# Modulation fillers placed otherwise: three in each mLSTM head, three in each RWKV pair

## What is computed

```
mod = silu(c) @ w_ada + b_ada            # six parts of 2048 columns each
h   = rmsnorm(x) * (1 + sc_a) + sh_a
z   = h @ w_in
y   = concat(rwkv7(z_a), mlstm(z_qk, z_rest)) @ w_out
x   = x + g_a * y
h   = rmsnorm(x) * (1 + sc_c) + sh_c
x   = x + g_c * peer(h)
mod = silu(c) @ w_ada_final + b_ada_final  # two more parts
y   = rmsnorm(x) * (1 + scale) + shift
```

## Time and profile before

| | us |
|---|---|
| median of 3 runs | 3099.91 |
| lowest and highest | 3097.11, 3103.96 |
| the profiled execution | 3092.3 |
| its span | 3090.5 |
| PE busy in the span | 2778.7 (90%) |
| POOL busy | 1741.7 (56%) |
| DVE busy | 1275.7 (41%) |
| ACT busy | 988.4 (32%) |

### The profile page before, as it was taken

The page is one execution under the profiler, slowest core; times in us unless marked ns, Lnnn a source line. Parts: engine busy times, 40 slices in busy tenths (PEclk is TensorE's granted clock), DMA queues, the critical chain, the costliest instruction groups (busy, mean ns, idle before and its releaser), DMA issues.

```text
span 3090.5 us, 57072 instructions
## 1 busy us (share of the span) xinstructions
PE 2778.7 (90%) x22999; PEld 2568.8 (83%) x22999; DVE 1275.7 (41%) x2183; ACT 988.4 (32%) x1350; POOL 1741.7 (56%) x719
## 2 busy tenths in 40 slices
PE   5689999958875979998999999899999899889997
PEld 1389996526653979998999899899999899889997
DVE  0350664464226640995788713200131201352233
ACT  1243432131102333444444333233333233223323
POOL 0167771002211757688455577677777677777774
PEclk9699997779986989999999999999999999999999
DMA  9534446966661434344444444455444454444442
GB/s 355 224 141 163 163 163 233 325 218 241 236 244 78 151 122 163 123 163 149 143 168 172 150 164 159 149 186 187 165 156 166 170 186 180 164 152 165 152 164 99
DMA packets 153351, 544.47 MB, mean 176 GB/s; under 512 B 9080, under 2 KB 22024, under 8 KB 124168
## 3 DMA queue, kind: packets, MB, share of 16 engines
q1 hardware_dynamic: 136384, 505.18, 46.0%
q10 hardware_dynamic: 14680, 20.41, 1.9%
q0 software_dynamic: 2160, 17.03, 1.3%
HBM read 518.74 MB, written 23.84 MB: 176 GB/s over the span
## 4 chain that ended last, share of the span: by engine, by line
issue 32%; POOL 28%; PE 25%; DVE 8%; DMA 5%; ACT 1%; POOLq 0%; SPq 0%; ACTq 0%; DVEq 0%
POOL ring_lo L561 28%; PE bank L627 25%; DMA kept<-in_w_ada 4%; DVE staged L1580 1%; DMA kept<-in_w_adaf 1%; DVE staged L1865 1%; DVE staged L1525 1%; DVE staged L1854 0%; ACT hi_front L1183 0%; DVE staged L1736 0%; ACT staged L1183 0%; DMA out_n_all<-staged 0%; DVE staged L1539 0%; POOLq L560 0%; DVE staged L1985 0%
## 5 line engine op out<-in xcount | busy, mean ns | idle before, releaser
L561 POOL TENSOR_TENSOR ring_lo<-kept,hi_peer 128x1024 fp32r<-128x1024 f32 x576 | 1444.4, 2530 | 623.8 <-ACT hi_peer L1183 623.8
L1183 ACT ACTIVATE hi_peer<-kept 128x1024 fp32r<-128x1024 f32 x576 | 578.9, 1053 | 1231.3 <-PE bank L627 1231.1
L627 PE MATMUL bank<-h_hi,ring_lo 128*128 128x288 f32 x3104 | 917.0, 295 | 0.0
L627 PE MATMUL bank<-h_hi,hi_peer 128*128 128x288 f32 x2304 | 690.3, 300 | 36.9 <-DVE staged L1865 15.9
L627 PE MATMUL bank<-h_lo,hi_peer 128*128 128x288 f32 x2304 | 684.1, 297 | 0.0
L627 PE MATMUL bank<-act_hi,hi_peer 128*128 128x288 f32 x2048 | 616.3, 301 | 41.0 <-POOL ring_lo L561 16.0
L627 PE MATMUL bank<-act_lo,hi_peer 128*128 128x288 f32 x2048 | 609.9, 298 | 0.0
L627 PE MATMUL bank<-act_hi,ring_lo 128*128 128x288 f32 x2048 | 609.7, 298 | 0.0
L627 PEld LDWEIGHTS bank<-h_hi,ring_lo 128*128 128x128 f32 x3104 | 589.2, 190 | 0.0
L627 PEld LDWEIGHTS bank<-h_hi,hi_peer 128*128 128x128 f32 x2304 | 436.4, 189 | 40.2 <-issue 35.7
L627 PE MATMUL bank<-staged 64*64 64x64 f32 (+10 forms) x5472 | 371.6, 268 | 91.6 <-issue 20.0
(11 more groups left out here) (186 smaller groups left out, 2442.5 us busy)
## 6 DMA issues: line engine op xcount, KB each, us to landing
kept<-in_peer_u SPq DMA_DIRECT2D x128, 1024.0 KB, 4.8
kept<-in_peer_v SPq DMA_DIRECT2D x128, 1024.0 KB, 5.6
kept<-in_w_ada SPq DMA_DIRECT2D x96, 1024.0 KB, 8.8
kept<-in_w_in SPq DMA_DIRECT2D x50, 1024.0 KB, 4.7
kept<-in_w_adaf SPq DMA_DIRECT2D x32, 1024.0 KB, 8.8
kept<-in_w_out SPq DMA_DIRECT2D x16, 1024.0 KB, 4.8
kept<-in_w_q SPq DMA_DIRECT2D x16, 1024.0 KB, 4.7
gates_spill<-staged ACTq DMA_DIRECT2D x32, 432.0 KB, 2.7
```

The source lines that it names most:

```text
L561: pool.tensor_tensor(ring_lo[:, n % RING_SLOTS, cols], ring[n % RING_SLOTS][:, cols], hi_slot(n)[:, cols].bitcast(F32), ALU.subtract).then ...
L627: return pe.matmul(out, lhsT, rhs, start=start, stop=stop)
L1183: return act.activation(out, in_, ACT.Copy)
```

## The change

In each head a third filler is put behind `ms_ready`, ahead of the state updates; on ScalarE its counterpart stands behind the root. In each pair the two fillers behind levels 1 and 3 become one behind level 2, and the one at the end of the pair is gone. The sum stays at 24, and the last stays in the sample part.

```diff
@@ TensorE, mLSTM head @@
                 for i in range(2):
                     mm = matmul(ps[0][:, 0:N], ones, hsq[:, i, :], i == 0, i == 1)
                 mm.then_inc(S("ms_ready"), 1)
+                ada_more(1)
 
                 pe.wait_ge(S("kwm_ready"), h + 1)
@@ TensorE, RWKV pair, levels of the doubling @@
                             times(q, q, X, Tt).then_inc(S("t_sum"), 1)
-                    if i == 1 or i == 3:
+                    if i == 2:
                         ada_more(1)
@@ TensorE, end of the pair @@
                     mm.then_inc(S("y_sum"), 1)
-                ada_more(1)
```

## The result

The kernel with the change takes 3116.86 us in the median of five runs (3111.45 to 3120.76), beside 3097.68 us for the kernel before (3096.22 to 3103.96). The ratio is 1.0052, with a 95% interval from 1.0037 to 1.0067: slower by 16 us. Two later series of the same kernel, each beside its own runs of before, gave 1.0083 (1.0067 to 1.0099, median 3124.4) and 1.0071 (1.0050 to 1.0092, median 3121.5). The change thus costs 16 to 26 us, and the forecast was +8. The direction was right, the first series lies in the range of 3098 to 3120, the medians of the two others just above it.

A forecast was written before the change was run, and what follows sets the result against it. It took waits for modulation-weight loads, a tile every 2.72 us, to bound the third fillers in the heads. Heads +44.0 and pairs -36.1 made +8 us, so 3108 us from a median of 3099.9; range 3098 to 3120.

The forecast's parts named there:

- The bound and the rate: Heads: a filler directly behind another waits for its tiles, landing every 2.72 us, and ends some 12 to 14 us later.
- The heads: Four third fillers ahead of the state updates delay them by 11.4, 11.3, 11.0 and 10.3 us, together 44 us.
- the clock rival: Heads: waits leave TensorE's clock low, each following head costs 3.5 us more, 10 together: 3118 us; chance 0.2.
- The fold "beside the loads, at nothing": Head 1, between second and third filler: the moved fold costs nothing beside the loads; 4.2 us without that cover.
- The pairs: RWKV pairs with four fillers less: -36.1 us together, bounds -31 to -38; pair 0 17 and pair 1 19 us shorter.
- the copy: End of pair 0: without the filler, the next products need only ScalarE's copy of the output, -7.2 us.
- the sample's filler: Behind pair 1: it still waits a little for tiles, ending near 903.8 against 918.90 us; 15.1 of 15.3 us kept.
- The other side: Rival in the heads: third fillers find their tiles and cost matmuls plus one fold, 19 to 26 us: 3085 to 3093; chance 0.1.
- Nothing to be seen: Rival: heads cost 40 us and pairs give 38, so 3102 us; chance 0.2.
- The signs: Expected in the trace: heads 10 to 12 us longer, last state near 669 us; new level 1 waits or numerators over 10 us refute.
- the 1.94 us that I called the lower clock: Heads: one tile's matmuls at the lower clock, upper end for the 1.5 us charged for the last tile.
- Behind the heads: Between the heads and the pairs: one filler and one fold beside the last state's stores, costed at nothing, perhaps a few microseconds.

The follow-up runs named there:

- Kept busy: Changed kernel plus two constant matmuls before the third filler's second to fourth tiles: heads 0 and 3, 3115.3 us (1.0067); heads 0, 2, 3, 3116.3 us (1.0054).
- the run of the pairs alone: Changed kernel without the heads' third fillers, four quarters of the modulation and their loads left out: 3059.1 us beside 3093.6 for the kernel before, ratio 0.9889.
- the run with unloaded fillers: Changed pairs, four quarters left out, plus 16 filler-shaped matmuls on constants per head at the third filler's place, no load: 3080.4 us.

## Why the prediction was right, and where its size was off

**The bound and the rate** were right for the gap between two fillers. The third filler's tiles arrived when the rows of before said (last group of head 0 at 526.39, predicted landing 526.9), and without a load the same matmuls cost the heads 16.4 us instead of 57.7.

**The heads: 44 us forecast, 57.7 measured in the first trace, 66.6 and 69.6 in the next two.** This is the term that was mis-sized. It ended at the start of the updates and took everything behind it as unchanged. The first series' 3116.9 lies nearer to the clock rival's 3118 than to the forecast of 3108. Per head the first trace has +14.5, +13.5, +14.5 and +15.2 against 11.4, 11.3, 11.0 and 10.3. In heads 0 and 3 the updates start 11.5 and 11.6 us later, counted from the head's start; the rest is the updates at 1.2 GHz, 9.23 us instead of 6.25 and 5.58. Kept busy, head 0 took 39.1 (37.4) and head 3 40.3 (43.8), where the forecast makes 38.1 and 40.7: in three of these four the sum without the clock holds within about 1 us. In head 2 the third filler ends where the forecast has it, within about 0.5 us once the fold that left the head's first filler is taken off, and the fold and the updates behind it make the difference (the kernel after, merged into one row; 4.2 and 5.71 us, 9.9 together, in the forecast):

```profile
619.46 12.95 PE L627 MATMUL bank<-staged 128*128 128x9 f32 x52
```

The 66.6 and 69.6 us of the later traces also hold more low clock ahead of the wait. Part of that spread comes without any third filler: the run of the pairs alone had heads of 130.6 us together, with two fillers, where the trace of before has 124.1.

**The fold "beside the loads, at nothing"** in head 1 failed in the same way, by its clock. TensorE's order of time in head 1, the kernel after:

```profile
562.63 1.06 PE L627 MATMUL bank<-kept,staged 128*32 128x512 f32 x8 [0.77 <-DMA kept<-in_w_ada]
563.62 5.79 PE L627 MATMUL bank<-staged 128*128 128x9 f32 x32
569.26 2.27 PE L627 MATMUL bank<-staged,kept 128*128 128x288 f32 x4
572.35 5.04 PE L627 MATMUL bank<-kept,staged 128*32 128x512 f32 x32 [0.82 <-issue]
577.32 5.59 PE L627 MATMUL bank<-staged 32*128 32x257 f32 x20
```

At the low clock the fold takes 5.79 us and the sum of squares 2.27 instead of 1.24. The filler no longer waits for tiles; its matmuls come in one piece behind the landed load and end 2 us later than they would have beside it. The pause of 0.82 us ahead of it, which the profile calls issue, fits the wait for the folded result that I had named: ScalarE's copy of it ends at 572.25.

**The clock as a rival** was named, with 3118, and it is what happened, at 13.7 us in the first trace instead of 10. I had given it 0.2 because the heads ran at the low level for part of their time before. That argument was weak: a stretch that is already slow in part leaves the rest to be lost. I had also put its price in the wrong place, the next filler and numerator, where it was the updates directly behind the wait. The Trainium skill ("TensorE: Matmul & The Clock Gate", section "HAM oscillation — how this bites in real kernels") describes waits for DMA between short bursts that send the engine back to its low clock; these traces agree, with a granted clock of 0.50 in the stretch behind the wait.

**The pairs: -36.1 forecast.** Measured -35.5 in the trace of that part alone; in the change -39.5 up to the sample products (19.0 in pair 0 and 20.5 in pair 1, forecast 17 and 19), with 2.1 given back. The parts stand: no wait opened behind the missing filler, the copy was next at the end of pair 0, and the sample's filler kept a small price.

**The other side** (a third filler that finds its tiles, 3085 to 3093) is what the run with unloaded fillers stands for: with free loads it came out below before, 3080 beside 3093.6, though 8 of these 13 us are the unexplained ones behind the start of `w_out`. With real loads it did not come. Its price was also added up wrongly: 19 to 26 against -36.1 makes 3083 to 3090, not 3085 to 3093. **Nothing to be seen** needed heads of 40.

**The signs.** The last state is handed to its store at 682.7 us instead of 625.3; I had said near 669. No new wait stands at the doubling's filler, and no numerator takes over 10 us (6.4 to 8.9). One reading of mine was loose: the 1.94 us that I called the lower clock stand where the profile gives a granted clock of 1.00 (from 36 to 40 us). Nearly the same, 1.93 us, stand at 526.39, where it gives 0.50, so the size holds; why the first row reads 1.00 stays open.

**Behind the heads** the stretch from head 3's end to the pairs was 98.0 us before and 98.2 after, so costing it at nothing was right.

## What to carry to other kernels

A filler has two prices, its matmuls and its bytes, and they are hidden in different places: look for a stretch where another engine is the bound *and* the transfers stand still. Count the bytes over the whole period of a loop, not over the gap between two fillers, and price them at the average rate of that period (here 300 to 330 GB/s), not at the rate of a full queue (385). A wait put ahead of small matmuls cost more than its length here, because what followed ran at half the clock; charge the work behind it at its low-clock duration.

## What the runs showed of the hardware that was not expected

- The same kernel's four heads took 181.8, 190.7 and 193.7 us in three executions, with the same matmuls at the low clock for more or less of their time (head 0's numerator 6.41 to 8.88 us), while the last tiles of heads 0 and 3 kept their distance of 2.7 us. The medians of its three series differ by up to 7.5 us.
- Six added matmuls per filler, 12 us of TensorE's time in two heads and work for nothing, went with 1.9 to 6.9 us less in these two heads, whichever traces with and without are compared.
- The clock also falls while TensorE is busy without a gap: in the kernel before it is 0.50 from 568 to 580 us, in the numerator of head 2 and the filler behind it, with PE busy for 4.00 of every 4.00 us. A wait is not the only thing that lowers it.
- With a state store and then a state load beside it, a tile takes 4.5 to 5.7 us instead of 2.7, at 337 to 419 GB/s for all together, as if the two kinds of transfer shared the rate about evenly.
- TensorE's pauses in the pairs that the profile puts down to nothing (0.2 to 2.2 us each) shift when code far ahead of them changes. With a lower clock beside them they ate 6 of 16 us in one run, 2.3 by the pauses. Their cause stays open.
